# Expert stage of a YOCO-style trunk: four 64-slot items for three, gate and up units by row chunk, one bank for transposes

## The reference, cut to what matters

```python
def swiglu(h, w_gate_up, w_down):
    g, u = jnp.split(h @ w_gate_up, 2, axis=-1)
    return (jax.nn.silu(g) * u) @ w_down

def moe(h, router, w_gate_up, w_down):
    ...
    top_p, top_i = lax.top_k(probs, TOP_K)
    top_p = top_p / jnp.sum(top_p, axis=-1, keepdims=True)
    gates = jnp.sum(jax.nn.one_hot(top_i, N_EXPERTS, dtype=jnp.float32) * top_p[..., None], axis=1)
    ...
    for e in range(N_EXPERTS):
        y = y + gates[:, e:e + 1] * swiglu(xt, w_gate_up[e], w_down[e])
```

## Time and profile before

| | us |
|---|---|
| median of 3 runs | 1203.26 (1202.20 to 1205.78) |
| the profiled execution, timed | 1204.16 |
| its span | 1202.4 |
| expert stage, from the first gather (443.2) to the last addition's end (1193.6) | 750.4 |
| PE busy | 1127.3 |
| mean granted clock of TensorE | 0.969 of 2.4 GHz |

### The profile page before, as it was taken

One profiled execution on the slowest core, in us unless ns is written; L12 is line 12 of the kernel. 1 busy time (PEld: TensorE's weight loads), 2 busy tenths in 40 slices (PEclk: granted clock), 3 DMA queues, 4 the chain that ended last, 5 costly groups with the idle time before them and its releaser, 6 DMA issues.

```text
span 1202.4 us, 15887 instructions
## 1 busy us (share of the span) xinstructions
PE 1127.3 (94%) x5499; PEld 845.2 (70%) x5499; DVE 703.8 (59%) x746; ACT 593.4 (49%) x627; POOL 14.0 (1%) x81
## 2 busy tenths in 40 slices
PE   7999999999999888999979999969999969999995
PEld 6867788888898776885337885337884337887884
DVE  6745555455654457983027973027973028978895
ACT  6444534334436536762026762126762126767773
POOL 1100000000000000000000000000000000000000
PEclk9879999999999979999989999989999989999998
DMA  9932456455455317998999999999999999999950
GB/s 354 313 105 84 162 176 205 179 175 205 148 179 169 106 35 241 363 366 299 390 397 387 391 396 366 392 396 387 392 395 349 392 396 387 393 394 336 379 206 35
DMA packets 166473, 343.23 MB, mean 285 GB/s; under 512 B 11869, under 2 KB 50826, under 8 KB 166410
## 3 DMA queue, kind: packets, MB, share of 16 engines
q1 hardware_dynamic: 166266, 341.93, 78.4%
q10 hardware_dynamic: 144, 0.52, 0.1%
HBM read 341.37 MB, written 1.05 MB: 285 GB/s over the span
## 4 chain that ended last, share of the span: by engine, by line
PE 78%; SPq 7%; DMA 5%; DVE 5%; issue 3%; ACT 2%; DVEq 0%; POOL 0%; POOLq 0%; ACTq 0%
PE ps L1396 22%; PE ps L1397 21%; PE ps L1398 21%; PE ps L1401 11%; SPq L327 7%; DMA raw<-moe_w_gate_up_dram 4%; DMA raw<-moe_w_down_dram 1%; DVE wlo L887 1%; PE ps L1710 1%; ACT whi L494 1%; DVE h L1069 1%; PE ps L1411 1%; DVE wlo L876 0%; DVE xlo L1112 0%; DVE h L1141 0%
## 5 line engine op out<-in xcount | busy, mean ns | idle before, releaser
L494 ACT ACTIVATE whi<-raw 128x2048 fp32r<-128x2048 f32 (+1 forms) x228 | 399.2, 1754 | 324.6 <-PE ps L1398 263.8
L887 DVE TENSOR_TENSOR wlo<-raw,whi 128x2048 fp32r<-128x2048 f32 x184 | 420.1, 2290 | 213.0 <-ACT whi L494 212.2
L1396 PE MATMUL ps<-whi,xhi 128*128 128x512 f32 (+1 forms) x744 | 298.3, 401 | 39.8 <-DVE xlo L1112 25.4
L1397 PE MATMUL ps<-whi,xlo 128*128 128x512 f32 (+1 forms) x744 | 291.9, 392 | 0.0
L1398 PE MATMUL ps<-wlo,xhi 128*128 128x512 f32 (+1 forms) x744 | 291.8, 392 | 0.0
L1396 PEld LDWEIGHTS ps<-whi,xhi 128*128 128x128 f32 x744 | 142.5, 192 | 77.1 <-DVE xlo L1112 28.1
L1398 PEld LDWEIGHTS ps<-wlo,xhi 128*128 128x128 f32 x744 | 142.5, 192 | 29.4
L1397 PEld LDWEIGHTS ps<-whi,xlo 128*128 128x128 f32 x744 | 142.8, 192 | 26.7
L1396 PE MATMUL ps<-whi,hhi 128*128 128x512 f32 x308 | 123.2, 400 | 0.0
L1397 PE MATMUL ps<-whi,hlo 128*128 128x512 f32 x308 | 121.7, 395 | 0.0
L1398 PE MATMUL ps<-wlo,hhi 128*128 128x512 f32 x308 | 121.6, 395 | 0.0
(11 more groups left out here) (282 smaller groups left out, 967.0 us busy)
## 6 DMA issues: line engine op xcount, KB each, us to landing
raw<-moe_w_gate_up_dram SPq DMA_DIRECT2D x352, 512.0 KB, 9.6
raw<-moe_w_down_dram SPq DMA_DIRECT2D x176, 512.0 KB, 11.2
raw<-ffn_w_gate_up_dram SPq DMA_DIRECT2D x44, 512.0 KB, 4.9
raw<-ffn_w_down_dram SPq DMA_DIRECT2D x22, 512.0 KB, 3.7
raw<-kv_shared_w_dram SPq DMA_DIRECT2D x16, 512.0 KB, 4.6
raw<-mla_w_o_dram SPq DMA_DIRECT2D x8, 512.0 KB, 14.3
raw<-sb_w_q_dram SPq DMA_DIRECT2D x8, 512.0 KB, 3.8
raw<-sb_w_o_dram SPq DMA_DIRECT2D x8, 512.0 KB, 3.7
```

The lines of the kernel that those rows point to most:

```text
L494: return nc.scalar.activation(o, i, ACT.Copy, scale=scale)
L887: V.tensor_tensor(wlo[:, s, :].rearrange("p a w -> p (a w)"), raw[:, (hh // 2) % RAW, :], whi[:, s, :].bitcast(F32).rearrange("p a w -> p ...
L1396: pe.matmul(o, a_hi, b_hi, start=start, stop=False, skip_group_check=True)
L1397: pe.matmul(o, a_lo, b_hi, start=False, stop=False, skip_group_check=True)
```

## The change

The fourth lightest expert becomes a small item too (`NS = 4`), and two of the small ones are last. The sequence is large, small, large, small, [overflow, if any, as large,] large, large, small, small. `rt_order` and the tables of items get 13 rows in this sequence.

Gate and up units are cut by row chunk. Unit x below 16 is row chunk x % 8 with gate and up of 1024 hidden columns, two transfers with pieces of 4 KB. Units 16 to 21 have the last 768 columns: three of them hold four row chunks, in 3, 4 and 3 transfers with pieces of 1 to 3 KB. In small items the four groups are 512, 512, 256 and 128 columns per array half.

In large items groups 0 and 1 are now made together by units 0 to 7, groups 2 and 3 by units 8 to 15, groups 4 and 5 by units 16 to 21. Group j has banks (0, 2, 4, 0, 2, 7)[j] and the next one. A new semaphore `even_done` marks the end of groups 0, 2 and 4. All transposes (hidden columns and `sel`) go to bank 6, behind units 9, 10, 17 and 18 and down units 1 and 2; each waits for the low part of the one before it. Down products go to banks 4 and 5, the gather to 6 and 7.

`begin` now waits for all of the next item's gathered tokens, transposes `sel`, and then makes two units of the next item instead of four. ScalarE copies the transpose to a new tile `selN`, and GpSimd multiplies that with itself into `selT` (it is 0 or 1), behind the former item's scatter.

```diff
-MW = 512
-MG = 6
-MU = (0, 4, 8, 12, 16, 20, 22)
+GU = 22
 SMALL = 64
-NS = 3
+NS = 4
 NB = N_EXP - NS
-ORDER = (0, 1, 4, 2, 5, 3, 6, 7)
+PAIRS = 2
 OVF = 5
...
+ORDER = (0, 1, 5, 2, 6, 7) + OVF * (-1,) + (3, 4)
+SUB = 6
...
+def sub_bank(j):
+
+    return (0, 2, 4, 0, 2, 7)[j]
...
+TR_BANK = 6
+
+
+def segments(x):
+
+    if x < 16:
+        return [(a * 1024, x % 8, a, x // 8 * 1024, 1024) for a in range(2)]
+    k, c = (x - 16) // 3 * 4, 2048
+    return (
+        [(0, k, 0, c, 768), (768, k, 1, c, 768), (1536, k + 1, 0, c, 512)],
+        [(0, k + 1, 0, c + 512, 256), (256, k + 1, 1, c, 768), (1024, k + 2, 0, c, 768), (1792, k + 2, 1, c + 512, 256)],
+        [(0, k + 2, 1, c, 512), (512, k + 3, 0, c, 768), (1280, k + 3, 1, c, 768)])[(x - 16) % 3]
...
+                if x < GU:
+                    for place, k, a, c, n in segments(x):
+                        sp_eng.dma_start(raw[:, u % RAW, place:place + n], w_gu[k * P:(k + 1) * P, a * FF + c:a * FF + c + n]
+                                         ).then_inc(landed[u % RAW], 16)
...
+            def scatter_weights(g):
+
+                pool.wait_ge(selN_ready, g + 1)
+                if not isinstance(g, int):
+                    pool.wait_ge(scattered, g * 4)
+                nc.gpsimd.tensor_tensor(selT[:, :], selN[:, :].bitcast(F32), selN[:, :].bitcast(F32), ALU.mult).then_inc(selT_ready, 1)
...
+                for x in range(2, FU):
+                    if x in (7, 15, 21):
+                        silu({7: 0, 15: 2, 21: 4}[x])
+                    if x in (10, 11, 18, 19, 24, 25):
+                        high({10: 0, 11: 1, 18: 2, 19: 3, 24: 4, 25: 5}[x])
...
+                    if x + 3 < FU or following == "big":
+                        split_high_unit(H_MOE + RING + 2 * x, i, g)
+                    if x in (7, 15, 21):
+                        silu({7: 1, 15: 3, 21: 5}[x])
...
+                        if k == 0 and j == 3:
+                            pe.wait_ge(gated[2], i * SUB + 1)
...
                 def transposes(j):
-                    pe.wait_ge(gated[2], i * MG + j + 1)
-                    if j >= 2:
-                        pe.wait_ge(h_lo[2], i * MG + j - 1)
-                    w = group_width(j)
+                    pe.wait_ge(gated[2], i * SUB + j + 1)
+                    if j >= 1:
+                        pe.wait_ge(h_lo[2], i * SUB + j)
+                    w = sub_width(j)
                     for b in range(w // P):
...
+                for x in range(2, GU):
+                    big_unit(x, i, g)
+                    if x in (9, 10, 17, 18):
+                        transposes({9: 0, 10: 1, 17: 2, 18: 3}[x])
...
-                    if d == 2:
-                        transposes(MG - 1)
...
+                    if d in (1, 2):
+                        transposes(d + 3)
```

More of the change, by code:

```diff
@@ L274, in moe_landed, with unit_raw, unit_split @@
         def moe_landed(x, g):
[L276 to L282, removed]
+            slot = (U_MOE + x) % RAW
+            of_slot = [n for n in range(FU) if (U_MOE + n) % RAW == slot]
+            a_unit = 32 * sum(u % RAW == slot for u in range(U_MOE))
+            within = 16 * sum(transfers(n) for n in of_slot if n <= x)
+            return landed[slot], g * (16 * sum(transfers(n) for n in of_slot)) + a_unit + within
+        def unit_raw(x):
+            return raw[:, (U_MOE + x) % RAW, :]
+        def unit_split(t, x):
+            r = (H_MOE + 2 * x) % RING
+            return t[:, r:r + 2, :].rearrange("p a w -> p (a w)")
         @block.sync
@@ L1169, in big @@
-                gate(MG - 1)
-                low(MG - 2)
-                for d in range(FU - MU[MG]):
-                    x = MU[MG] + d + RING // 2
-                    if d == 10:
+                for x in range(2, FU):
+                    if x in (7, 15, 21):
+                        gate({7: 0, 15: 2, 21: 4}[x])
+                    if x in (10, 11, 18, 19, 24, 25):
+                        low({10: 0, 11: 1, 18: 2, 19: 3, 24: 4, 25: 5}[x])
+                    if x == 14:
+                        item_gates(g, row)
+                        choose(g + 1, next_row, following)
+                    if x == FU - 1:
@@ L1180, in big @@
[L1180 to L1182 removed]
+                    if x + 3 < FU or following == "big":
+                        split_low_unit(H_MOE + RING + 2 * x, i)
+                    if x in (7, 15, 21):
+                        gate({7: 1, 15: 3, 21: 5}[x])
+                    if x == 29 and following == "big":
                         gathered_low(i + 1)
                 if following == "big":
[L1185 removed]
+                    for x in range(3, 5):
@@ new lines, in small_unit @@
+            def small_unit(x, p, g):
+                pe.wait_ge(*moe_landed(x, g))
+                r = unit_raw(x)
+                if x < 16:
+                    k = x % 8
+                    if x < 8:
+                        pe.wait_ge(xs_ready, p * KD + k + 1)
+                    for a in range(2):
+                        for n in range(2):
+                            w = slice(a * 1024 + n * 512, a * 1024 + (n + 1) * 512)
+                            last = mm(ps[n * SMALL:(n + 1) * SMALL, 2 * (x // 8) + a, :], xs[:, k, :], r[:, w], k == 0, k == KD - 1)
+                else:
+                    if x == 16:
+                        pe.wait_ge(small_gated, p * SMALL_GROUPS + 1)
+                    for j in (4, 5):
+                        half = sub_width(j) // 2
+                        for place, k, a in pieces(x, j):
+                            for n in range(2):
+                                w = slice(place + n * half, place + (n + 1) * half)
+                                last = mm(ps[n * SMALL:(n + 1) * SMALL, j - 4, a * half:(a + 1) * half], xs[:, k, :], r[:, w],
+                                          k == 0 and a == 0, k == KD - 1)
+                last.then_inc(small_used, 1)
```

486 lines of the change are left out of this document (241 added, 245 removed).

## The result

The changed kernel takes 1218.84 us (median of 4 runs, 1216.58 to 1220.29), the kernel before 1204.52 (4 runs): a ratio of 1.0118, with a 95% interval of 1.0092 to 1.0145. The prediction had 1200.8 and a range up to 1216. The profiled execution spans 1216.0 us, where the working of the prediction ended at 1199.9: 16.1 us have to be found. Eight items ran, so there is no overflow item.

A forecast was written before the change was run, and what follows sets the result against it. PE was taken to bound large items, transfers small ones. First cut 558.0, small legs 73.2, large legs lengthened by 7.9 and the last two small items summed to 1199.9; taken from the median, 1200.8 us, range 1176 to 1216.

The forecast's parts named there:

- rival at 0.10: Large items: the clock falls to 1.2 GHz at each of twelve new PE waits, + 20 us, 1221; chance 0.10.
- The small leg of 73.2: Small item behind a large one: 71.3 us from landings plus 1.9 is 73.2, against 75.0 and 76.0 before.
- the last two small items: End of the expert stage: two small items in a row, 148.3 us until their last unit lands at 1184.6.
- PE binds: Large items of the kernel before: PE busy for 95.5 of 96.7 us, so PE's work sets their time.
- 1.9 us "missing": Small leg: the sum at old rates gave 73.1 where 75.0 was measured; the 1.9 was added to 71.3.
- the old 4.9: End of a small item: 4.9 us from the second unit's landing to PE's start on the next item.
- The waits, + 7.9: Each large leg: 0.6 for matmuls, 6.2 for three waits on the low part, 1.1 in unit 8.
- the rival at 0.18: New gate and up transfers miss their packets' rate; small legs lengthen by 10 us, 1205 to 1211; chance 0.18.
- The swap: Order of items: a small leg in the place of a large one is worth 104 - 73 = 31 us.
- The first gap: First large item: PE's 3.3 us gap for unit 3's split goes, 2.8 us off; first cut at 558.0.
- the overflow item: Routing differs from the reference, one token more makes an extra large leg of some 110: 1311; chance 0.04.

The follow-up runs named there:

- e9: Kernel before, with gathered tokens taken ahead of the splits of the next item's first two units at a small item's end: 1200.29 us, ratio 0.9972.
- e11: Changed kernel with second transposes one unit later, gathered tokens ahead of the splits, and four small-item units ahead of the scatter: 1171.73 us, ratio 0.9740.
- e1: Changed kernel with the second transposes of each pair, and their copies, one unit later: 1184.70 us, ratio 0.9828 to the kernel before.
- e3: Kernel before with four small items in the sequence of the changed kernel, nothing else: 1184.32 us, ratio 0.9829.
- e2: Changed kernel with three small items and the sequence of before: 1250.22 us, ratio 1.0371 to the kernel before.
- e4: Changed kernel with units 0 to 15 in four transfers with 2 KB pieces instead of two with 4 KB: 1224.44 us, ratio 1.0160.

## Why the prediction was wrong

Two steps of the sum failed. The low clock behind the new waits had no term in it (it was a rival at 0.10) and cost 10 us. The small leg of 73.2 measured 77.0 and 77.2, and the last two small items, worked out in the same way, came out 2.5 longer than forecast: 10.3 us. The other terms come out within 3 us each and nearly cancel.

- **What bounds the kernel.** "PE binds" in large items, transfers in small ones: true of each row by itself and wrong of the kernel. The cuts gave legs of 103.3 and 76.0, and their sum, 179.3, is little more than the 176.4 us that 66 units need at the rates of the earlier trace rows; I never added them. The second and third small leg had no length of their own there (e9), so they could not tell what one would be after the change. No wrong term of the sum comes from this, since the small leg was added up from landings; it hid what a gain in one stage is worth.
- **The small leg, 73.2.** Its sum took the first slot's load at 7.0 us, the full rate from there, and then 1.9 us "missing", from a leg of the kernel before whose queue had run just as dry (85 GB/s in both). But that leg had four units ahead of the scatter and the changed one has two, and the restart costs more: measured 1.9 more up to the second landing (1.0 of it by the scatter's place, by e11; the other 0.9 stays open), and 1.9 more from there to PE's start, where the prediction took the old 4.9 although it had said that PE now waits for all tokens. The last two items are 2.5 longer than forecast; they begin with the same restart (their first 3.7 us have 71 GB/s).
- **The waits, + 7.9.** Right in place, number and size: 1.92 to 1.98 for 2.05, and 1.0 for 1.1. e1 without them has no stretch of low clock in a large item.
- **The clock.** A rival at 0.10, priced right (1.7 for 1.6 us each), and it happened at six of twelve: 10 us. Five of the six fall in the three large legs of the table: without them these would have come out 2.4 us under the forecast, with them 5.6 over. The only evidence used against it was that waits of 1.2 us in all did no harm, which says nothing of waits of 2. "TensorE: Matmul & The Clock Gate" of the Trainium skill, section "HAM oscillation — how this bites in real kernels", describes a kernel in which every wait, of some 3 to 5 us, brings the low clock; the waits here are of 1.9 to 2.0 us, and half of them did.
- **The transfers of the new units.** 409 GB/s where the queue is full and gate and up units of 4 KB pieces land, and 397 for the mixed ones (1156 to 1172 us): right, and the rival at 0.18 is out. It just mattered little.

```profile
1125.00:1150.00 25.00, 20.06 (x86) 5.22 (x82) 1.12 (x3) 1.19 (x2) 0.00 (x0) 1.00 1.03 409
```

- **The swap.** A small leg for a large one was said to be worth 31 us, which four times 7.9 take away. With the units of before it is worth 21 (e3), inside the changed kernel 31 (e2).
- **The first gap.** 558.0 and 558.25, by luck: the stage began 2.8 us sooner, and from its first gather on the term is 3.1 us short, 1.6 of it a fall of the clock.

The chances: 0.86 lay on cases up to 1211. Only two rivals reached further: the overflow item, which did not come, and the clock, to 1221, but with twelve falls; with the six that came it gives 1210 or 1211. The measured 1218.8 needed them and longer small legs together, and no case held both.

## What to carry to other kernels

Add up neighbouring stages and compare the sum with the transfers' time: if the sum fits while each stage seems to have its own limit, the transfers set the pace, and a gain at one stage counts once. When a change makes one stage slower than the loads behind it, the ring fills and the queue stops: price the restart, not only the rate. And where two products of a chain of three engines share one bank, put a full turn of the chain between them; one unit more of distance was worth 34 us here.

## What was not expected of the hardware

Idle times of 1.92 to 1.98 us in an otherwise full TensorE were followed by about 3.4 us at 1.2 GHz in six cases of twelve, idle times of 1.0 us never. In e1, without these waits, there was none inside a large item beyond its start.

The three runs that have these waits (the changed kernel, e2 and e4) show a pattern. They have 13 large items with three waits each. Behind the first wait of an item the clock fell every time, 13 of 13. Behind the second it fell in 5 items, and behind the third in the same 5: 23 falls in 39 waits. The place alone does not fix it: the last large item has one fall in the changed kernel and three in e4, at the same places. Nor does the length of the idle time: the 13 idle stretches of 2.03 to 2.21 us behind the scatter were never followed by a fall. What decides stays open: no run was made on it.
